# Weight units signalled in four pieces, and the norm's sums placed later, at the head of a two-layer decoder trunk on one core

## What is computed

```
h = concat(meta, x)                                   # 16 + 512 = 528 tokens, 1024 channels
for l in range(2):
    hn = rms_norm(h, norm_g[l]);  z = hn @ w_in[l]
    (x_rnn, g_rnn, sc_b, sc_c, x_sc, g_sc, c_q, c_kv, k_rope, g_att, gate_logits) = split(z)
    y_rnn = (rg_lru(x_rnn, ...) * silu(g_rnn)) @ rg_out[l]
    y_sc  = (sc_b * causal_conv(sc_c * x_sc) * silu(g_sc)) @ sc_out[l]
    y_att = (mla(c_q, c_kv, k_rope, ...) * silu(g_att)) @ mla_out[l]   # norms c_q and c_kv first
    g = sigmoid(gate_logits + gate_b[l])
    h = h + (g[0]*y_rnn + g[1]*y_sc + g[2]*y_att) @ w_out[l]
return h[:, 16:]
```

## Time and profile before

| | |
|---|---|
| median of 3 executions | 1707.57 us (1707.35 to 1708.2) |
| the profiled execution | 1710.33 us, of which the profile's span is 1708.5 us |
| granted TensorE clock, mean | 0.998 of full speed |
| PE busy | 1692.2 us, 99% of the span |
| POOL busy | 1205.5 us, 71% |
| DVE busy | 880.7 us, 52% |
| ACT busy | 479.9 us, 28% |

### The profile page before, as it was taken

How to read it: one execution, slowest core, us unless ns; L and a number is a source line. 1 busy time by engine, 2 the same in 40 slices (tenths; PEclk the granted TensorE clock), 3 DMA queues, 4 the chain that set the end, 5 groups by cost and what they waited for, 6 DMA issues and landing times.

```text
span 1708.5 us, 31580 instructions
## 1 busy us (share of the span) xinstructions
PE 1692.2 (99%) x11624; PEld 1572.8 (92%) x11624; DVE 880.7 (52%) x1263; ACT 479.9 (28%) x867; POOL 1205.5 (71%) x1365
## 2 busy tenths in 40 slices
PE   7999999999999999999999999999999999999999
PEld 7999999999999999999998888888888888888887
DVE  7966758485545452212348757484846445322221
ACT  4423333332322331101125333333323313301110
POOL 7764848485688777777766748484866898777773
PEclk9999999999999999999999999999999999999999
DMA  4431222122232233222432312221222322423233
GB/s 158 138 101 63 92 72 81 66 92 81 93 104 80 86 109 114 86 90 92 153 129 76 111 58 97 71 92 58 92 98 85 98 90 86 145 86 98 92 118 113
DMA packets 49406, 164.16 MB, mean 96 GB/s; under 512 B 6048, under 2 KB 7456, under 8 KB 49056
## 3 DMA queue, kind: packets, MB, share of 16 engines
q1 hardware_dynamic: 41328, 146.56, 25.8%
q10 hardware_dynamic: 8032, 17.00, 2.9%
HBM read 152.21 MB, written 10.81 MB: 95 GB/s over the span
## 4 chain that ended last, share of the span: by engine, by line
PE 90%; DVE 6%; issue 2%; ACT 1%; DMA 0%; DVEq 0%; ACTq 0%
PE slots L516 79%; PE slots L581 3%; PE slots L615 3%; PE slots L677 2%; PE slots L599 1%; DVE early L1278 1%; DVE early L1293 1%; PE slots L550 1%; DVE qr_hi_and_lo L1110 1%; PE slots L566 1%; DVE kr_lo L1110 1%; DVE kn_lo L1110 1%; DMA residual_or_merged<-xt 0%; DVE branch_lo L1123 0%; DVE early L1300 0%
## 5 line engine op out<-in xcount | busy, mean ns | idle before, releaser
L428 POOL TENSOR_TENSOR w_lo<-w_raw,w_hi 128x256 fp32r<-128x256 f32 x1004 | 842.0, 868 | 20.9
L423 POOL TENSOR_SCALAR w_hi<-w_raw 128x1024 fp32r<-128x1024 f32 x251 | 290.0, 1155 | 335.5 <-PE slots L516 326.4
L516 PE MATMUL slots<-h_hi,w_hi 128*128 128x264 f32 (+1 forms) x2112 | 520.5, 310 | 0.7 <-DVE sc_pad L1406 0.7
L516 PE MATMUL slots<-h_lo,w_hi 128*128 128x264 f32 (+1 forms) x2112 | 515.4, 308 | 0.0
L516 PE MATMUL slots<-h_hi,w_lo 128*128 128x264 f32 (+1 forms) x2112 | 514.7, 308 | 0.0
L516 PEld LDWEIGHTS slots<-h_hi,w_hi 128*128 128x128 f32 x2112 | 342.7, 188 | 21.1 <-issue 1.6
L516 PEld LDWEIGHTS slots<-h_hi,w_lo 128*128 128x128 f32 x2112 | 341.7, 188 | 19.1
L516 PEld LDWEIGHTS slots<-h_lo,w_hi 128*128 128x128 f32 x2112 | 342.0, 188 | 18.2
L516 PE MATMUL slots<-branch_hi,w_hi 128*128 128x264 f32 (+1 forms) x552 | 143.5, 319 | 11.1 <-DVE branch_lo L1123 9.2
L516 PE MATMUL slots<-branch_lo,w_hi 128*128 128x264 f32 (+1 forms) x552 | 142.2, 317 | 0.0
L516 PE MATMUL slots<-branch_hi,w_lo 128*128 128x264 f32 (+1 forms) x552 | 141.7, 316 | 0.0
(11 more groups left out here) (237 smaller groups left out, 2732.0 us busy)
## 6 DMA issues: line engine op xcount, KB each, us to landing
w_raw<-w_units SPq DMA_DIRECT2D x251, 512.0 KB, 3.3
stream<-sc_acc ACTq DMA_DIRECT2D x16, 264.0 KB, 2.1
sc_back<-stream SPq DMA_DIRECT2D x2, 2112.0 KB, 8.0
x_old<-stream SPq DMA_DIRECT2D x16, 264.0 KB, 4.4
stream<-residual_or_merged ACTq DMA_DIRECT2D x16, 264.0 KB, 2.4
ab_raw<-w_units SPq DMA_DIRECT2D x8, 512.0 KB, 4.1
residual_or_merged<-xt ACTq DMA_DIRECT2D x4, 528.0 KB, 7.9
stream<-xt ACTq DMA_DIRECT2D x1, 2112.0 KB, 11.7
```

The source lines that it names most:

```text
L423: pool.tensor_scalar(hi, raw, 1.0, 1.0, ALU.mult, ALU.mult).then_inc(sem("hi_part"), 1)
L428: op = pool.tensor_tensor(lo[:, cols], raw[:, cols], hi[:, cols].bitcast(F32), ALU.subtract)
L516: mm = pe.matmul(out[:, a_, 0:t1 - t0], w(k), x(k)[:, t0:t1], start=(n == 0), stop=(n == 3 * ks - 1))
```

## The change

Units 1 and 2 of layer 0 are now also split in four pieces that signal one by one (`PIECEWISE = 3`), and PE waits for them by pieces. In layer 0, `stat` moves from behind the second k-tile of q0 to behind the sixth, and `spread` from before kr to behind kr's fifth k-tile; layer 1 keeps its order (`STAT_AT`, `SPREAD_AT`). The four halvings of the biases move on DVE from ahead of the norm's reciprocals to behind the last `h_lower`, ahead of `q_lower(1)`.

```diff
+PIECEWISE = 3
+STAT_AT, SPREAD_AT = (6, 2), (5, 0)
...
-            def split_first():
+            def split_first(j):
                 width = UNIT // LO_PIECES
                 for n in range(LO_PIECES):
                     cols = slice(n * width, (n + 1) * width)
-                    if n == 0:
+                    if j == n == 0:
                         pool.wait_ge(sem("first_in"), 16)
-                    if n == LO_PIECES // 2:
-                        pool.wait_ge(sem("unit_in0"), 16)
-                    pool.tensor_scalar(w_hi[0][:, cols], w_raw[0][:, cols], 1.0, 1.0, ALU.mult, ALU.mult).then_inc(
-                        sem("first_hi"), 1)
-                    pool.wait_ge(sem("first_hi"), n + 1)
-                    pool.tensor_tensor(w_lo[0][:, cols], w_raw[0][:, cols], w_hi[0][:, cols].bitcast(F32),
+                    elif n == (0 if j else LO_PIECES // 2):
+                        pool.wait_ge(sem(f"unit_in{j % STAGING}"), 16 * (j // STAGING + 1))
+                    pool.tensor_scalar(w_hi[j][:, cols], w_raw[j % STAGING][:, cols], 1.0, 1.0, ALU.mult,
+                                       ALU.mult).then_inc(sem("first_hi"), 1)
+                    pool.wait_ge(sem("first_hi"), LO_PIECES * j + n + 1)
+                    pool.tensor_tensor(w_lo[j][:, cols], w_raw[j % STAGING][:, cols], w_hi[j][:, cols].bitcast(F32),
                                        ALU.subtract).then_inc(sem("first_split" if n < LO_PIECES - 1 else "unit_split"), 1)
...
-                    split_first()
-                for j in range(l == 0, 6):
+                    for j in range(PIECEWISE):
+                        split_first(j)
+                for j in range(PIECEWISE if l == 0 else 0, 6):
                     split_unit("CQ", l, 0, j)
...
-                first = stage == "CQ" and l == j == 0
-                hi, lo = (pieces_of(0) if first else unit_ready(stage, l, i, j))
+                first = stage == "CQ" and l == 0 and j < PIECEWISE
+                hi, lo = (pieces_of(j) if first else unit_ready(stage, l, i, j))
                 for k in ks:
                     if first and k < KT - 2:
-                        pe.wait_ge(sem("first_split"), k // 2 + 1)
+                        pe.wait_ge(sem("first_split"), (LO_PIECES - 1) * j + k // 2 + 1)
...
-                latent("q0", 2, range(0, 2))
+                latent("q0", 2, range(0, STAT_AT[l]))
...
-                latent("q0", 2, range(2, KT))
+                latent("q0", 2, range(STAT_AT[l], KT))
+                if SPREAD_AT[l]:
+                    latent("kr", 3, range(0, SPREAD_AT[l]))
                 out = free("NORM", l, 0, "spread")
                 spread(l, out, n_diag, lambda t: at("n_diag", l, 0, t + 1)).then_inc(sem("norm_mm"), 1)
-                latent("kr", 3)
+                latent("kr", 3, range(SPREAD_AT[l], KT))
...
-            for l0 in range(DEPTH):
-                for first, count in ((BA, 2), (GB0, 3)):
-                    c = (l0 * NPARAM + first) * KT
-                    dve.tensor_scalar(pv[:, c:c + count * KT], pv[:, c:c + count * KT], 0.5, None,
-                                      ALU.mult).then_inc(sem("biases_halved"), 1)
-
             for l in range(DEPTH):
...
                 h_lower(7)
+                if l == 0:
+                    for l0 in range(DEPTH):
+                        for first, count in ((BA, 2), (GB0, 3)):
+                            c = (l0 * NPARAM + first) * KT
+                            dve.tensor_scalar(pv[:, c:c + count * KT], pv[:, c:c + count * KT], 0.5, None,
+                                              ALU.mult).then_inc(sem("biases_halved"), 1)
                 q_lower(1)
```

## The result

| | before | changed |
|---|---|---|
| median, runs taken in turns (7 of each) | 1707.43 us (1707.22 to 1709.89) | 1712.45 us (1711.49 to 1714.15) |
| profiled execution, span | 1710.33, 1708.5 us | 1711.49, 1709.7 us |
| POOL, DVE busy | 1205.5, 880.7 us | 1207.9, 876.3 us |

The changed kernel is slower: the ratio is 1.0026 with an interval of 1.0016 to 1.0036, or 4.4 us; the medians lie 5.0 apart. The forecast was 1708.0 and the range ended at 1709.9, so both were wrong. The profiled execution of the changed kernel is the lowest of its runs, and that of before lies 2.9 above the median in the table, which is why the two profiled times are only 1.2 apart: what the two traces show up to the loop must be read step by step, not as the whole difference.

A forecast was written before the change was run, and what follows sets the result against it. PE, busy 99% of the span, was taken as the bound. Its lead at kr's end (−1.3), the kv diagonal wait (+1.0) and the q2 square wait (+0.7) gave +0.4 us: 1708.0 us, range 1706.1 to 1709.9.

The forecast's parts named there:

- The stall before kv1: PE's 1.88 us idle between kv0 and kv1, waiting for POOL's unit 1; forecast to go, kv1 starting at 16.6 to 17.4.
- the diagonal: At spread_kv, PE was to wait for DVE's kv diagonal from 45.0 until 46.0, a term of +1.0 us.
- the square: At stat_q, PE was to stand 0.8 us for ACT's square of q2, a term of +0.7 us in the sum.
- the 1 us allowed: Sign of being right: stat_q on PE begins within 1 us of 54.29.
- the slower rival: POOL's pieces of units 1 and 2 alternate with DVE's sums, 2.6 us a piece: +2.5 us, 1710.1; chance 0.15.
- PE's stall before kr: At kr's first product, PE was to wait 1.3 us for unit 3, ready at 31.6.
- the very number of the forecast: The forecast's sum at stat_q: PE 0.4 us later than in the kernel before.
- The extra waits of PE by pieces cost nothing: On PE, waiting piece by piece was to add nothing, since kv0 has such waits and keeps 0.73 us a k-tile.
- Everything later is unchanged code … I carry the 0.4 through: After stat_q, the code is unchanged, so the +0.4 us reached there was carried unaltered to the end.
- 0.2% as the frame for "no change": Whole kernel: a change over 0.2% needs more than 3.4 us; staying within 0.2% was given 0.94.
- the chance of 0.04 for slower: Whole kernel slower by over 0.2%: needs the second rival and the dearest halvings together; chance 0.04.
- the signs of being wrong: No stall before kr, stat_q before 53.5, pieces over 2.3 us, kr begun past 33, or a difference only after 60 us.

The follow-up runs named there:

- experiment 11: The changed kernel again, unedited, against the kernel before on the same chip: 1713.24 us, ratio 1.0023.
- experiments 3 and 4: The kernel before with 14, and with 7, always-met waits added on PE ahead of the loop: 1711.85 us, ratio 1.0018, and 1712.67 us, 1.0019.
- experiment 2: The change with its waits kept but the loop's head not pinned: 1710.99 us, ratio 1.0010 to the kernel before.
- experiments 1 and 2: The change without the repeated waits: 1711.04 us, ratio 1.0011; the change with waits, head not pinned: 1710.99 us, 1.0010; both ratios to the kernel before.
- experiment 7: The kernel before with only the four halvings moved as in the change: 1710.63 us, ratio 1.0009.
- experiment 8: The kernel before with only `stat` behind q0's sixth k-tile and `spread` behind kr's fifth: 1711.57 us, ratio 1.0015.
- experiment 5: The kernel before once more, unedited, as a control: 1708.50 us, ratio 0.9995.

## Why the prediction was wrong

**Right.** The stall before kv1 went. A piece beside DVE took 1.98 us (taken: 2.08), DVE's sums ended at 22.4 (taken: 22.3). DVE began its h tiles late, PE waited at spread_kv for the diagonal and at stat_q for the square, and stat_q came at 53.65 on PE's timeline (54.22 before) and at 54.59 in experiment 11, within the 1 us allowed. Strict turns of POOL and DVE, the slower rival, did not happen: the prediction worked them out at 5.2 us for two pieces and four instructions of DVE, 2.6 us a piece, and the rows show 1.98.

**Sizes.** Unit 1 was ready at 19.84, not 21.4, since its first piece began at 11.90 instead of 13.08: 0.7 us of that came with an earlier landing of the first weights (5.56, before 6.24). In experiment 11, where they landed at 6.42, it was ready at 21.23, near the 21.4 taken. Unit 3 took 3.9 us and not 4.5, because the diagonal began only at 29.03, when POOL was nearly through; PE's stall before kr was 0.2 instead of 1.3. `Spread` ended at 34.65 instead of 36.4, so DVE began at 34.69, 0.2 us later than before and not 2.0. The kv diagonal fell beside POOL's unit and took 1.79, and PE waited 1.7 for it instead of 1.0. The halvings cost 0.86 from start to start, not 0.6. Up to stat_q these errors cancelled, partly by luck: PE was 0.6 us ahead of before in this pair of traces, and in experiment 11, with the later weights, 0.4 behind the same trace, the very number of the forecast.

**The steps that failed.** First, "The extra waits of PE by pieces cost nothing": they cost nothing where they stand (in the change the k-tiles of kv1 follow each other at 0.73 us), but 344 and 351 instructions ahead of the pinned loop bring a stall at its entry that 337 and 338 do not. Where they are the only thing changed it costs 0.0018 to 0.0019 of the time (experiments 3 and 4, 3.1 to 3.2 us); on top of DVE's late COPY it costs 0.0013 to 0.0016 (the change against experiment 2, 2.2 to 2.7 us), the same within the scatter. Of that 1.6 to 2.0 us is the stall itself, and the rest goes with the lower clock. The place to look at was not in the trace but in the code: `head_slot` on the loop.

Second, "Everything later is unchanged code … I carry the 0.4 through": the path by which DVE frees slot 2 for `va` had nothing to spare. In the change the COPY ends 2.89 us after stat_q's start instead of 1.74, 1.15 later, mostly because `kv_lo` now runs beside POOL. Without the stall at the loop's head (experiments 1 and 2) `va` begins 3.02 us after stat_q instead of 1.88, 1.14 more, of which the profile counts 1.03 as idle. I had followed only PE's needs up to stat_q, one step short of where they met DVE. The ratios put the whole of what is left without the stall at 0.0010 to 0.0011 (experiments 1 and 2); the halvings alone gave 0.0009 (experiment 7) and the order alone 0.0015 (experiment 8), which do not add up and need not, since either alone already pushes `kv_lo` beside POOL.

Third, 0.2% as the frame for "no change" rested on the idle that could be won (1.9 us). An edit can also add idle, and the chance of 0.04 for slower had counted only known waits. None of the signs of being wrong looked at the loop's entry.

**Open.** How much of the remaining 0.0010 of experiments 1 and 2 is wait and how much clock differs from execution to execution and cannot be told from the single traces. Why the stall at the loop's head comes on top of the wait for the COPY, and does not run beside it, is not explained. What PE stands for at the entry was not shown, and a version with `head_slot` at another value than 0 was not tried.

## What to carry to other kernels

When a kernel pins a loop's head, count the instructions ahead of it before adding even free ones, waits included (here 338 brought no stall, and 344 one of 2.0 us), and look at the packets of the instruction queue after (28 without the stall, 29 with it). When work is moved, follow every engine's run to the next buffer that it frees, and read there how long after the freeing instruction the waiting engine starts: here PE never began `va` less than 0.13 us after the COPY's end, so the 0.14 us before it was not slack. Moving small instructions off one place puts them in front of something else, and what they push may land beside a busy neighbour at twice its time (`kv_lo` took 2.54 us in experiment 7 instead of 1.31).

## What the runs showed of the hardware

Entering the loop after 344 or 351 instructions, with its head pinned, cost 1.6 and 2.0 us of idle PE, and 2.6 and 2.9 where a wait of 1.0 for VectorE came with it, and one more packet in the instruction queue; after 337 or 338 instructions, or with the same waits and the head not pinned, neither appeared. PE started `va` 0.13 to 0.14 us after the end of the VectorE COPY that released it. `kv_lo`, two DVE instructions of 128x528, took 1.31 to 1.32 us where POOL's next unit began only in its last 0.4 us, and 2.15 to 2.54 where that unit began before it or within its first 0.3 us. Short pieces on POOL, in turn, leave DVE more than long instructions do: its seven sums took 7.2 us (15.21 to 22.41) beside pieces, 1.03 each, against 8.4 and 1.20 beside whole units. And the granted clock fell to 0.50 for 3.4 to 13.6 us of a trace, the last few us of the span left out, in stretches of 3.4 and 6.8 at a few places (the loop's entry and about 917 us among them). Executions of one kernel have more or fewer of them (both of these places in the first trace of before, only the second in that of experiment 5). The time goes with the mean clock in this kernel, whose PE is busy for 99% of the span: the 33 runs of before on one chip spread from 1705.7 to 1711.5, those with a mean clock of 0.997 at 1711.3 and those with 1.000 at 1706.7.
